# A decoder layer on one core: value weights loaded behind the diagonal blocks, and half of the inverse's round trip on ScalarE's queue

## The reference

```python
diff = gc[..., :, None] - gc[..., None, :]
decay = jnp.where(causal, jnp.exp(jnp.where(causal, diff, 0.0)), 0.0)
A = jnp.where(strict, jnp.einsum('nbhid,nbhjd->nbhij', kb, k) * decay, 0.0)
L = A + jnp.eye(C, dtype=A.dtype)
sol = lax.linalg.triangular_solve(L, rhs, left_side=True, lower=True, unit_diagonal=True)
u, w = sol[..., :DV], sol[..., DV:]
def chunk_step(S, inp):
    v_new = u_n - jnp.einsum('bhck,bhkv->bhcv', w_n, S)
    o_n = jnp.einsum('bhck,bhkv->bhcv', q_n, S) + jnp.einsum('bhij,bhjv->bhiv', qk_n, v_new)
    S = S * ge[..., None, None] + jnp.einsum('bhck,bhcv->bhkv', k_n, v_new)
```

## Time and profile before

| | us |
|---|---|
| median of 3 runs | 2575.93 |
| lowest and highest of them | 2569.89 and 2577.12 |
| the profiled execution | 2577.91 |
| its span, first to last instruction | 2576.2 |
| stage of the prompt's 8 heads, about | 100 to 911 |
| from one head's end to the next (SP's issue of S, L548, second to third head) | 97.4 |

### The profile page before, as it was taken

One profiled execution on the slowest core, in us unless ns is written; L12 is line 12 of the kernel. 1 busy time (PEld: TensorE's weight loads), 2 busy tenths in 40 slices (PEclk: granted clock), 3 DMA queues, 4 the chain that ended last, 5 costly groups with the idle time before them and its releaser, 6 DMA issues. The chain is left out here.

```text
span 2576.2 us, 35779 instructions
## 1 busy us (share of the span) xinstructions
PE 2247.1 (87%) x13120; PEld 1956.5 (76%) x13121; DVE 1543.4 (60%) x2042; ACT 1141.1 (44%) x1614; POOL 369.4 (14%) x391
## 2 busy tenths in 40 slices
PE   4688898899898679899879999969759999999990
PEld 2388888888888567778679999958648888888870
DVE  2355655655655542266744545436569898898985
ACT  3233343343343230154533334333237777787764
POOL 1002202202202212122300000020021111111103
PEclk8799999999999886799989999989869999999995
DMA  8510210210210132620055555553279999999956
GB/s 336 182 43 20 68 51 19 68 51 19 68 51 20 36 88 71 210 61 3 4 167 149 144 151 151 150 186 115 89 270 391 402 404 403 405 401 404 409 222 229
DMA packets 310883, 432.17 MB, mean 168 GB/s; under 512 B 57698, under 2 KB 251730, under 8 KB 290755
## 3 DMA queue, kind: packets, MB, share of 16 engines
q1 hardware_dynamic: 289788, 369.53, 41.3%
q0 software_dynamic: 11296, 39.46, 4.1%
q10 hardware_dynamic: 9720, 22.11, 2.2%
HBM read 375.98 MB, written 57.10 MB: 168 GB/s over the span
## 5 line engine op out<-in xcount | busy, mean ns | idle before, releaser
L2645 DVE TENSOR_TENSOR ex_w_r<-ex_w,ex_wh 128x2048 fp32r<-128x2048 f32 x198 | 447.1, 2287 | 61.5 <-ACT ex_wh L2587 61.4
L2587 ACT ACTIVATE ex_wh<-ex_w 128x2048 fp32r<-128x2048 f32 x198 | 379.1, 1917 | 120.3 <-PE ex_up L2542 41.4
L2015 DVE TENSOR_TENSOR mg_w_r<-mg_w,mg_wh 128x1024 fp32r<-128x1024 f32 x94 | 115.0, 1225 | 131.7 <-ACT mg_wh L1977 131.7
L1977 ACT ACTIVATE mg_wh<-mg_w 128x1024 fp32r<-128x1024 f32 x94 | 99.5, 1059 | 175.6 <-DVE mg_out L2040 92.1
L894 PE MATMUL gd_ps<-hh,gd_wh 128*128 128x352 f32 x368 | 122.9, 334 | 10.7 <-ACT preS L614 10.7
L1964 PE MATMUL mg_psum<-hh,mg_wh 128*128 128x352 f32 x384 | 125.1, 326 | 1.7 <-PEq L1728 1.7
L1964 PE MATMUL mg_psum<-hh,mg_w_r 128*128 128x352 f32 x384 | 124.6, 325 | 0.0
L1964 PE MATMUL mg_psum<-mg_xh,mg_wh 128*128 128x352 f32 x384 | 124.0, 323 | 0.4 <-DVE mg_w_r L2015 0.2
L1964 PE MATMUL mg_psum<-hT_r,mg_wh 128*128 128x352 f32 x384 | 124.3, 324 | 0.0
L1964 PE MATMUL mg_psum<-mg_xh,mg_w_r 128*128 128x352 f32 x384 | 123.5, 322 | 0.0
L894 PE MATMUL gd_ps<-hh,gd_w_r 128*128 128x352 f32 x368 | 118.3, 321 | 0.0
(11 more groups left out here) (636 smaller groups left out, 6023.2 us busy)
## 6 DMA issues: line engine op xcount, KB each, us to landing
ex_w<-in_w_gate_dram SPq DMA_DIRECT2D x66, 1024.0 KB, 8.0
ex_w<-in_w_up_dram SPq DMA_DIRECT2D x66, 1024.0 KB, 7.6
ex_w<-in_w_down_dram SPq DMA_DIRECT2D x66, 1024.0 KB, 8.6
ada_w<-in_w_ada_dram SPq DMA_DIRECT2D x24, 1024.0 KB, 15.9
mg_w<-in_w_in_dram SPq DMA_DIRECT2D x48, 512.0 KB, 3.8
expert_out_scratch<-ex_y ACTq DMA_DIRECT2D x33, 512.0 KB, 7.6
gd_w<-in_w_in_dram SPq DMA_DIRECT2D x32, 512.0 KB, 4.8
mg_w<-in_w_br_gdn_dram SPq DMA_DIRECT2D x24, 512.0 KB, 3.7
```

What stands on the lines that cost most here:

```text
L1977: nc.scalar.activation(wh[q][:], wl[q][:], ACT.Copy).then_inc(w_high, 1)
L2015: nc.vector.tensor_tensor(wl_r[q][:], wl[q][:], wh[q][:].bitcast(F32), ALU.subtract).then_inc(w_low, 1)
L2587: nc.scalar.activation(wh[at][:], wl[b][u][:], ACT.Copy).then_inc(w_high, 1)
L2645: nc.vector.tensor_tensor(wl_r[b][u][:], wl[b][u][:], wh[at][:].bitcast(F32), ALU.subtract).then_inc(w_low, 1)
```

## The change

Three things are moved, all in `delta_prompt`, and no arithmetic is touched. The load of the next head's value weights, with its wait for `v_proj`, goes from ahead of the two stores of `AT` to behind the load of `Ab`. The store of `YbT` and the two loads of `YT` go from SP to ScalarE, behind `high(3, i + 1)` and ahead of the tanh of the values, each with the wait it had.

```diff
@@ block.sync, body
                         sp.wait_ge(z_proj, i * 3 + 3)
                         load(3, i + 1)
-                        sp.wait_ge(v_proj, i * 3 + 3)
-                        load(2, i + 1)
                     for g in range(2):
                         sp.wait_ge(ats, i * 8 + g * 4 + 4)
                         sp.dma_start(image(c.at_s, g), v4(AT[g][:])).then_inc(at_out, 16)
                     sp.wait_ge(at_out, i * 32 + 32)
                     sp.dma_start(Ab[:], diagonal(c.at_s)).then_inc(blocks_in, 16)
+                    if nxt:
+                        sp.wait_ge(v_proj, i * 3 + 3)
+                        load(2, i + 1)
                     sp.wait_ge(solved, i + 1)
                     sp.dma_start(diagonal(c.y_s), Yb[:]).then_inc(y_out, 16)
-                    sp.dma_start(diagonal(c.yt_s), YbT[:]).then_inc(y_out, 16)
                     sp.wait_ge(y_out, i * 32 + 32)
                     for g in range(2):
                         sp.dma_start(v4(Y[g][:]), image(c.y_s, g)).then_inc(y_in[g], 16)
-                        sp.dma_start(v4(YT[g][:]), image(c.yt_s, g)).then_inc(y_in[g], 16)
@@ block.scalar, body
                         evac(0, 2, i + 1)
                         high(3, i + 1)
+                    act.wait_ge(solved, i + 1)
+                    act.dma_start(diagonal(c.yt_s), YbT[:]).then_inc(y_out, 16)
+                    act.wait_ge(y_out, i * 32 + 32)
+                    for g in range(2):
+                        act.dma_start(v4(YT[g][:]), image(c.yt_s, g)).then_inc(y_in[g], 16)
                     act.wait_ge(v_conv, i * 4 + 4)
                     act.wait_ge(z_silu, i + 1)
                     nc.scalar.activation(th[2][:], y[2][:], ACT.Tanh, scale=0.5).then_inc(v_tanh, 1)
```

## The result

| | before | after |
|---|---|---|
| median of 12 runs each, us | 2571.84 | 2557.40 |
| lowest and highest | 2561.04 and 2580.02 | 2551.32 and 2563.52 |
| ratio, 95% interval | | 0.9945 [0.9932, 0.9959] |
| span of the profiled execution | 2576.2 | 2561.8 |
| first projection of the heads to the last store of S | 111.78 to 909.54: 797.76 | 116.13 to 895.23: 779.10 |

The change makes the kernel faster by 14.4 us in the medians; 2557.5 was forecast. The stage of the heads is 18.66 us shorter in the profiled executions, and what follows them agrees within 0.1 us in these two. Ahead of it this execution lost 4.35 us: the heads began at between 110.8 and 116.1 us in the ten profiles of this study, with no code changed ahead of them. What follows the heads, where no code is changed either, took between 1657.4 and 1666.6 us in the ten.

What follows compares the result with a forecast made beforehand. TensorE was taken as bound by the chain AT, DRAM, blocks, solve, DRAM, Y. Terms 12.4 + 3.2 + 0.8 + 2.0 = 18.4 us off 2577.91 gave 2559.5, less 1.98 for the median: 2557.5; 8-in-10 range 2543 to 2570.

Steps and rivals of the forecast that it cites:

- The stores of `AT`: Before the solve: blocks asked for 2.34 us after AT is complete, VectorE's wait gone, solve 4.8 us earlier in the third head.
- `YbT` late on ScalarE, 12.4 us left: After the solve: ScalarE issues YbT only after high(3); loads still go out 1.77 us earlier in each of seven heads.
- Loads side by side, 3.2 us: Loads of Y and YT from two queues: first pair saves 0.45 us of issue in each of seven heads.
- The last head, 0.8 us: Head without next weights: 0.63 us between the two stores and 0.45 of the loads, taken as 0.8 won.
- The clock, 2.0 us: From the doubling's start to the first subtraction: bounds 8 us lost to 11 won over seven heads, 2 taken as won.
- The rival of the kept clock: TensorE starts the doubling at 2.4 GHz in all seven heads: nine us more gain, 2548 us; chance 0.16.
- VectorE's half us: VectorE's step after ScalarE's tanh, delayed by the moved loads, comes at most half a us later a head; taken as nothing.

Runs made afterwards that it cites:

- e1: Only the value weights' load moved, with the store of YbT and loads of YT back on SP, against the kernel before: 2541.43 us, ratio 0.9867.
- e5: The changed kernel plus 13 unused matmuls filling TensorE's gap ahead of the doubling: 2539.39 us, ratio to before 0.9858.
- the second execution: The changed kernel run once more, unaltered, for a second profile: 2559.16 us, ratio to before 0.9931.
- e6: Kernel with only the value weights moved, their load now put between the stores of AT and the load of the blocks: 2543.32 us, ratio to before 0.9870.
- e3: The changed kernel with ScalarE's store of YbT ahead of the last projection copy and high(3), loads of YT left in place: 2536.06 us, ratio to before 0.9860.

## Why the prediction was right, and where its steps were not

Sign and mechanism were right. The sum was 18.4 us, and the heads got 18.66 shorter in the first execution and 15.4 in the second. That the sum comes so near is partly luck, as terms that were mis-sized cancel in it. That 2557.5 meets 2557.40 is luck too: the sum was taken off a median of three runs, 2575.93, and the median of twelve is 2571.84, so that this comparison shows 14.4 us. The later one shows 2577.51 - 2559.16 = 18.35.

- **The stores of `AT`**: as forecast. 2.3 us from `AT` to the blocks, VectorE's wait gone in seven heads.
- **`YbT` late on ScalarE, 12.4 us left**: the cause was right, the place wrong. I put the issue behind `high(3)`, and it came 1.2 us sooner (384.83 instead of 386.07), when the wait of the copy before was met. That an engine works its instructions in order, as I had it, doesn't hold for this DMA: it went out ahead of an activation that stands before it. TensorE's gaps shrank by 35.94 - 16.46 = 19.5 us, against 12.4 + 3.2 = 15.6. By e1 the late pair still costs 18.6 us: 16.46 - 5.46 = 11.0 in TensorE's gaps, 47.9 - 42.5 = 5.4 in the stretch to the subtraction, and the rest in what follows, where the clock is lost around the scores in four heads instead of two. I had seen the first of these and not the two others.
- **Loads side by side, 3.2 us**: wrong in sign for the first pair, which the term is about. From the issue of the loads to the doubling it takes 3.89 us on one queue (398.37 - 394.48; 3.87 in e1) and 4.19 on two (391.56 - 387.37). So the term is about -2. What failed is the half of the issue time that I counted as won: side by side, each load takes longer to land. The rows are the DMA issues (KB each, median us from issue to landing), first of the changed kernel, then of e1, which has one queue:

```profile
gd_Y<-y_block_scratch SPq DMA_DIRECT2D x16, 256.0 KB, 4.2
gd_YT<-yt_block_scratch ACTq DMA_DIRECT2D x16, 256.0 KB, 4.8
```

```profile
gd_Y<-y_block_scratch SPq DMA_DIRECT2D x16, 256.0 KB, 3.6
gd_YT<-yt_block_scratch SPq DMA_DIRECT2D x16, 256.0 KB, 4.0
```

  The Trainium skill ("DMA: Bandwidth & Descriptors", section "Issuing engines are not separate DMA queues") was right that no rate is to be had there; by these rows not even the time to issue came back for the first pair. The second pair did come sooner. Its products start 393.37 - 387.37 = 6.00 us after the first load's issue, and 400.96 - 394.48 = 6.48 before; that half us is in the stretch to the subtraction and not in this term:

```profile
400.96 2.07 PE L915 MATMUL gd_x<-gd_Y,gd_am 128*128 128x128 f32 x8 [0.52 <-DMA gd_YT<-yt_block_scratch]
```

- **The last head, 0.8 us**: 0.1 (13.1 us from `Yb` to the first subtraction before, 13.0 after). `YbT` was issued with `Yb`, but the loads went out 3.27 us later as with one queue.
- **The clock, 2.0 us**: 49.6 - 47.9 = 1.7 won, though in another way than I saw. The clock is up when the doubling starts and falls within the first two us. The rival of the kept clock didn't come, and e5 shows what it would have brought: 14 us, not the 9 that I gave it. The Trainium skill ("TensorE: Matmul & The Clock Gate", section "Why this matters for your kernels") advises short gaps so that the clock isn't lost. Gaps of 2.2 to 2.5 us were too long here in all 14 heads of two executions.
- **Not foreseen**: two more falls ahead of the scores, each about 1.65 us (from the scores to the gap ahead of the doubling 27.4 to 27.5 us with a fall, 25.8 without), -3.3 us.

19.5 + 1.7 + 0.1 - 3.3 = 18.0, against 18.66 measured. For the second execution the same terms give 19.4 + 0.5 + 0.0 - 5.0 = 14.9, against 15.4. VectorE's half us didn't bind: it waits 1.28 to 2.71 us for the subtraction in the seven heads. Why the gap of 1.9 us ahead of the scores loses the clock in some heads and not in others is open; it happened in 2, 4 and 5 of 7 heads in three executions of two kernels with the same work ahead of it, and in 2, 0, 1, 2, 5 and 2 in e1 to e6.

## What to carry to other kernels

Price the two halves of a change alone and together. Here one half alone was worth 37 us of the heads and the other alone 8, but together they brought 18.7, because the first half brings the solve forward to a time at which ScalarE is still waiting. The sum looked like a modest success. When a DMA is moved to another engine's queue, ask which semaphore that engine waits for just ahead of it: here this wait, and not the engine's busy time, delayed the DMA and all that waited for it. When a gap of TensorE shrinks from 5 us to 2, read the clock in the us after it, and not just in its first products.

## What was not expected of the hardware

- ScalarE issues a DMA while the activations ahead of it still run or wait their turn: 384.83 against 385.01 for the start of `high(3)`, and moving it ahead of `high(3)` gained 0.1 of 1.06 us.
- Loads of 256 KB that two queues issue side by side each land later (4.2 and 4.8 us after their issue) than those that one queue issues in turn (3.6 and 4.0 in e1). The last of a head's four lands 5.9 us after the first issue, and 6.15 with one queue (means over seven heads of the changed kernel and of e1).
- After a gap of 2.2 to 2.5 us TensorE's clock was at 2.4 GHz in the first us of the products and fell to 1.2 GHz in the second, in 14 of 14 heads; with gaps of 0.7 to 1.3 us (e1, e3) it fell in six of 14, 2.0 to 3.3 us after the products' start.
